# Expert weights laid out by numpy, so that each half slot is one transfer of 1 MB

## The reference

```
logits = (t @ w_router).astype(jnp.float32)
top_val, top_idx = lax.top_k(logits, TOP_K)
...
for e in range(N_EXPERTS):
    out = out + gates[:, e:e + 1] * swiglu(t, e_gate[e], e_up[e], e_down[e])
```

## Time and profile before

| What | Before |
|---|---|
| median of 3 runs | 2481.01 us (2480.24 to 2481.51) |
| profiled execution: its time, its span | 2482.85 us, 2481.6 us |
| mean granted TensorE clock | 0.994 |
| TensorE matmul busy | 2404.3 us, 97% |
| TensorE weight load busy | 1709.1 us, 69% |
| VectorE, ScalarE busy | 1046.6 us (42%), 808.7 us (33%) |
| DMA packets, bytes | 335229, 641.30 MB, mean 258 GB/s |
| expert loads, us from issue to landing | 10.9 to 13.4 (512 KB), 12.6 and 13.9 (1024 KB) |

### The profile page before, as it was taken

How to read it: one execution, slowest core, us unless ns; L and a number is a source line. 1 busy time by engine, 2 the same in 40 slices (tenths; PEclk the granted TensorE clock), 3 DMA queues, 4 the chain that set the end, 5 groups by cost and what they waited for, 6 DMA issues and landing times.

```text
span 2481.6 us, 37133 instructions
## 1 busy us (share of the span) xinstructions
PE 2404.3 (97%) x16044; PEld 1709.1 (69%) x16044; DVE 1046.6 (42%) x1477; ACT 808.7 (33%) x1107; POOL 140.4 (6%) x144
## 2 busy tenths in 40 slices
PE   9999999999999988999959999999999999999998
PEld 7899886442444433444318987898988988798897
DVE  6755563010101101010116558757547546666544
ACT  5444352010010100010114435644444444644442
POOL 2200130000000000000000001000000003400000
PEclk9999999999999999999989999999999999999999
DMA  7665468999999999999995644446556546265651
GB/s 269 207 212 181 155 216 321 377 367 394 394 394 394 394 394 393 393 392 394 392 378 165 204 137 152 168 143 232 188 171 220 187 155 252 95 228 186 205 192 46
DMA packets 335229, 641.30 MB, mean 258 GB/s; under 512 B 15701, under 2 KB 128513, under 8 KB 334673
## 3 DMA queue, kind: packets, MB, share of 16 engines
q1 hardware_dynamic: 330208, 618.64, 69.4%
q0 software_dynamic: 4848, 20.20, 2.4%
HBM read 637.73 MB, written 1.05 MB: 257 GB/s over the span
## 4 chain that ended last, share of the span: by engine, by line
PE 83%; DMA 6%; SPq 5%; DVE 4%; ACT 1%; issue 1%; POOL 0%; DVEq 0%
PE bank L640 17%; PE bank L642 17%; PE bank L641 17%; PE bank L1412 11%; PE bank L1465 6%; PE bank L1430 5%; SPq L569 5%; DMA raw_hi<-in_exp_w_down_dram 3%; PE bank L1488 2%; DVE part_lo L588 1%; PE bank L1076 1%; PE bank L1047 1%; DMA turned_raw<-in_w_in_dram 1%; PE bank L1450 1%; PE bank L652 1%
## 5 line engine op out<-in xcount | busy, mean ns | idle before, releaser
L588 DVE TENSOR_TENSOR part_lo<-raw,part_hi 128x2048 fp32r<-128x2048 f32 x149 | 339.0, 2290 | 185.6 <-ACT part_hi L580 185.6
L640 PE MATMUL bank<-x_hi,turned_part_hi 128*128 128x256 f32 x1440 | 401.7, 279 | 0.0
L641 PE MATMUL bank<-x_lo,turned_part_hi 128*128 128x256 f32 x1440 | 398.9, 277 | 0.0
L642 PE MATMUL bank<-x_hi,turned_part_lo 128*128 128x256 f32 x1440 | 398.9, 277 | 0.0
L580 ACT ACTIVATE part_hi<-raw 128x2048 fp32r<-128x2048 f32 x149 | 281.5, 1908 | 45.7 <-DMA raw<-in_ffn_w_up_dram 35.3
L640 PEld LDWEIGHTS bank<-x_hi,turned_part_hi 128*128 128x128 f32 x1440 | 270.8, 188 | 6.3 <-issue 3.0
L641 PEld LDWEIGHTS bank<-x_lo,turned_part_hi 128*128 128x128 f32 x1440 | 271.0, 188 | 3.2
L642 PEld LDWEIGHTS bank<-x_hi,turned_part_lo 128*128 128x128 f32 x1440 | 270.5, 188 | 0.0
L588 DVE TENSOR_TENSOR turned_part_lo<-turned_raw,turned_part_hi 128x2048 fp32r<-128x2048 f32 x98 | 223.5, 2311 | 89.7 <-ACT turned_part_hi L580 88.6
L2699 DVE TENSOR_TENSOR h<-silu,bank 128x256 f32<-128x256 f32 x56 | 23.6, 421 | 501.5 <-ACT silu L2011 501.5
L1412 PE MATMUL bank<-raw_hi,expert_in 128*64 128x512 f32 x896 | 212.0, 594 | 10.8 <-DMA raw_hi<-in_exp_w_up_dram 10.8
(11 more groups left out here) (292 smaller groups left out, 3268.4 us busy)
## 6 DMA issues: line engine op xcount, KB each, us to landing
raw<-in_exp_w_gate_dram SPq DMA_DIRECT2D x112, 512.0 KB, 11.9
raw<-in_exp_w_up_dram SPq DMA_DIRECT2D x112, 512.0 KB, 13.4
raw_hi<-in_exp_w_gate_dram SPq DMA_DIRECT2D x112, 512.0 KB, 10.9
raw_hi<-in_exp_w_up_dram SPq DMA_DIRECT2D x112, 512.0 KB, 12.3
raw<-in_exp_w_down_dram SPq DMA_DIRECT2D x56, 1024.0 KB, 12.6
raw_hi<-in_exp_w_down_dram SPq DMA_DIRECT2D x56, 1024.0 KB, 13.9
raw<-in_ffn_w_down_dram SPq DMA_DIRECT2D x55, 1024.0 KB, 4.9
turned_raw<-in_ffn_w_gate_dram SPq DMA_DIRECT2D x70, 512.0 KB, 4.1
```

What stands on the lines that cost most here:

```text
L588: p.nc.vector.tensor_tensor(p.part_lo[t][i][:, :], p.raw[t][i][:, :], p.part_hi[t][i][:, :].bitcast(F32), ALU.subtract).then_inc(*self.spl ...
L640: nc.tensor.matmul(out, stat_hi, move_hi, start=start, stop=False, skip_group_check=True)
L641: nc.tensor.matmul(out, stat_hi, move_lo, start=False, stop=False, skip_group_check=True)
L642: return nc.tensor.matmul(out, stat_lo, move_hi, start=False, stop=stop, skip_group_check=True)
```

## The change

numpy lays the expert weights out before the program is built. `exp_w_up` now holds gate and up together as [expert, chunk, quarter, partition, 2048], and `exp_w_down` is [expert, chunk, half, partition, 2048]. The 2048 numbers are in the order in which the half slot holds them, so a load is one transfer with 8192 contiguous bytes per partition, and the 1 MB of a load is one contiguous stretch of HBM. `exp_w_gate` is no input any more. The bytes, the order of the loads, the slots and all work of the engines are as before.

```diff
-    def expert_part(self, w, q, row, cols):
+    def expert_part(self, w, q, part):
         i, p = q // NQ, self.p
         if i % N_EXP == 0:
-            return w[0][0][row:row + 256, cols].rearrange("(k p) n -> p k n", p=P)
+            return w[0, q % NQ, part]
...
-        return w[0, bass.ds(self.expert[i], 1), row:row + 256, cols].rearrange("o (k p) n -> p (o k) n", p=P)
+        return w[bass.ds(self.expert[i], 1), q % NQ, part].rearrange("o p n -> p (o n)")
...
         def up(q):
-            cols = slice(q % NQ * FE, (q % NQ + 1) * FE)
             for kq in range(4):
-                self.add((st, "up", q, kq),
-                         [(part, lambda w=w, row=kq * 256: self.expert_part(w, q, row, cols))
-                          for part, w in (("wide_gate", a["exp_w_gate"]), ("wide_up", a["exp_w_up"]))])
+                self.add((st, "up", q, kq), [("half", lambda kq=kq: self.expert_part(a["exp_w_up"], q, kq))])
...
-                         [("rows", lambda q=q, d=d: self.expert_part(a["exp_w_down"], q, q % NQ * FE + d * 256, slice(0, D)))])
+                         [("half", lambda q=q, d=d: self.expert_part(a["exp_w_down"], q, d))])
...
+def gate_up_by_chunk(gate, up):
+    both = np.stack([gate[0], up[0]]).reshape(2, N_EXP, 4, 2, P, NQ, FE)
+    return np.ascontiguousarray(both.transpose(1, 5, 2, 4, 3, 0, 6)).reshape(N_EXP, NQ, 4, P, SLOT)
...
+def down_by_chunk(down):
+    rows = down[0].reshape(N_EXP, NQ, 2, 2, P, D)
+    return np.ascontiguousarray(rows.transpose(0, 1, 2, 4, 3, 5)).reshape(N_EXP, NQ, 2, P, SLOT)
```

More of the change, by code:

```diff
@@ L557, in fetch @@
                 p.sp.wait_ge(*p.t.at(*self.before[name]))
-            wide = raw[:, :].rearrange("p (k m n) -> p k m n", k=2, m=2)
             views = {
@@ L562, in fetch @@
                 "up": raw[:, :].rearrange("p (k m n) -> p k m n", k=4, m=2)[:, :, 1, :],
-                "wide_gate": wide[:, :, 0, :], "wide_up": wide[:, :, 1, :],
+                "half": raw[:, :],
                 "rows": raw[:, :].rearrange("p (j n) -> p j n", j=2),
@@ L617, in landed_up @@
         raw, landed = self.where(name)
-        self.p.pe.wait_ge(*landed.at(name, "wide_up"))
+        self.p.pe.wait_ge(*landed.at(name, "half"))
         return raw[:, :].rearrange("p (k m n) -> p k m n", k=2, m=2)
@@ L624, in landed_down @@
         raw, landed = self.where(name)
-        self.p.pe.wait_ge(*landed.at(name, "rows"))
+        self.p.pe.wait_ge(*landed.at(name, "half"))
         return raw[:, :].rearrange("p (j n) -> p j n", j=2)
@@ L3158 @@
 _INS = ["x", "w_in", "gm_ws", "gm_bs", "gm_ln_g", "gm_ln_b", "gla_wa2", "gla_ba", "gla_norm_g", "w_out", "ln_mix_g",
-        "ln_mix_b", "ffn_w_gate", "ffn_w_up", "ffn_w_down", "router_w", "exp_w_gate", "exp_w_up", "exp_w_down",
+        "ln_mix_b", "ffn_w_gate", "ffn_w_up", "ffn_w_down", "router_w", "exp_w_up", "exp_w_down",
         "ln_ffn_g", "ln_ffn_b", "mem_2", "ln_g_2", "ln_b_2", "ffn_w_gate_2", "ffn_w_up_2", "ffn_w_down_2",
@@ L3186 @@
             a = np.ascontiguousarray(np.asarray(inputs[name])[0].T.reshape(KT, P, T).transpose(1, 0, 2))
+        elif name == "exp_w_up":
+            a = gate_up_by_chunk(np.asarray(inputs["exp_w_gate"]), np.asarray(inputs[name]))
+        elif name == "exp_w_down":
+            a = down_by_chunk(np.asarray(inputs[name]))
         elif name == "gm_ws":
```

## The result

The changed kernel takes 2436.23 us (median of 4 runs, 2433.33 to 2438.21) against 2481.09 us before (median of 4 runs on the same chip, 2480.24 to 2481.51). The ratio is 0.9819, with a 95% interval of 0.9802 to 0.9836: faster by 44.9 us, or 1.8%. The forecast was 2434.0, range 2427 to 2452. The profiled execution took 2434.55 us (span 2433.3), which is 48.3 us less than the one of before. Executions of one kernel differ by up to 5 us, so I break down the 48.3, and take 44.9 as the gain.

The account below looks back on a forecast made before the run. Expert-load DMA was taken to bound lean experts and the stage's end, TensorE the full experts. Loads at 2.52 instead of 2.68 us save 47.1 us: 2481 - 47 = 2434 us, range 2427 to 2452 for 8 in 10.

Parts of the forecast that it names:

- What bounded the kernel: Expert stage: DMA queue bounds lean experts and the stage's end; TensorE bounds full experts at 16.24 us a chunk.
- The price: Time per 1 MB expert load: 2.68 us before, 2.52 with the change, ends 2.49 and 2.55.
- slips: Expert loads: 0.02 us added to the mean load price for instruction loads and slips between.
- the direct rows of `mem`: Two `mem` loads with 8 KB rows, at 420 and 415 GB/s: 2.50 and 2.53 us for 1 MB.
- the rule weighed: Trainium skill's fixed 3 cycles per packet: an estimated 2.44 us per MB in 8 KB rows, sum 2428; not adopted.
- The ledger: Chunk-by-chunk account of the expert stage from load price and TensorE work: stage ends at 1251.6 us, 47.1 sooner.
- The edits costed at nothing: Expert stage: 224 fewer SP issues, one landing wait per half slot and more MB queued were counted as free.
- A wait of 13 us may still do that: Stage's end: the `hT` wait may still lower TensorE's clock and slow matmuls; 2 us counted on both sides.
- Rows above 4 KB gaining nothing: Rival for expert loads: 8 KB rows go like the downs, 2.57 us a load, 33 us saved, 2448; chance 0.14.
- That row length is no limit: Rival for expert loads: some common port gives 393 GB/s whatever comes, time 2481; chance 0.05.
- Reads within one contiguous MB getting in each other's way: Slower rival for expert loads: 16 engines conflict, 377 GB/s, 2.78 us a load, 26.7 us later, 2508; chance 0.05.
- TensorE bounding it all: Rival for the expert stage: loads at 2.44 us or under, 53 us and more saved, 2428 or less; chance 0.06.

Follow-up runs that it names:

- half the bytes: Changed kernel, but behind the first 18 loads each expert load brings only half its numbers, all matmuls kept, results wrong: 2418.47 us, ratio 0.9744.
- the first experiment: Changed kernel, still one transfer of a contiguous MB per load, but 2 KB rows for ups and 4 KB for downs: 2482.61 us, ratio 0.9999 to the kernel before.
- the last two changes tried: Changed kernel with half of each later expert load: 2418.47 us; changed kernel with dense-load rounding and subtraction moved later, rounding behind the last `hT` copies: 2424.26 us.
- the new order: Changed kernel with ScalarE's rounding of dense loads behind the last `hT` copies and VectorE's subtraction behind the first rows' normalisation: 2424.26 us, ratio 0.9765.

## Why the prediction was right

**What bounded the kernel.** Right. The lean experts lost their waits, the full experts kept their 16.24 us, and with half the bytes chunk 55 starts no sooner. The leads say it most directly. By the landing times, the first load of chunk 28 was there 28.6 us ahead of its use (15.5 before, forecast 28 and 16). At the end of lean expert 4 it was 8.2 us (0 before, forecast 7), and ahead of expert 7 it was 31.1 (14.8 before, forecast 28). With 4 KB rows the lead is 0 at the end of experts 4 and 7.

**The price.** Right. 2.50 for a load in the stream, 2.52 with slips were taken; the trace has 2.49 at 421 GB/s and 2.53 from the queue's bytes, and landings 2.52 us apart. The step from the difference of 2 and 4 KB rows holds over the whole span:

| bytes in a row | packets per engine and MB | GB/s | us per MB | 2.39 + 0.010 x packets |
|---|---|---|---|---|
| 1 KB | 64 | 348 | 3.01 | 3.03 |
| 2 KB (up loads before) | 32 | 387 | 2.71 | 2.71 |
| 4 KB | 16 | 409 | 2.56 | 2.55 |
| 8 KB | 8 | 421 | 2.49 | 2.47 |

(The 2 KB row is worked out from the starts in rows 4; the others are rates of a full queue. us per MB is 1.048576 MB by GB/s.) The slope from the ends is (3.01 - 2.49) / 56 = 0.0093 us, so the line from two points was steeper by 7% than this, and the direct rows of `mem`, which I preferred to its 2.47, were nearer. Against the rule weighed: 9.3 ns a packet are 2.6 times the 3 cycles of the Trainium skill's "DMA: Bandwidth & Descriptors", Why small descriptors are slow (an estimate of 3.5 ns at the page's 850 MHz), so the trace goes against it for this queue. What a packet's fixed time is spent on, no run here shows.

**The ledger.** Right in kind, with its terms off by 1 to 4 us, which partly cancel. Its "expert 1 begins at 519.3 as now" was wrong: it begins at 515.8 (517.0 when run again). Its chunk 55, 702.0 us later, is 704.5 us later in the trace. Of these 2.5 us, 0.5 are in expert 1. From chunk 14 to 55 the ledger has 622.9; the kernel with half the bytes, which hardly waits for loads, took 624.2 (597.3 to 1221.5), so TensorE's own time was summed 1.3 us too short; and the changed kernel took 624.9 (595.4 to 1220.3), 0.7 more. The wait for `hT` came at 14.0 where 13 stood. The stage ends at 1251.4 (forecast 1251.6), because these errors cancel: that part of the closeness is luck. The parts that the forecast names, 39.5 and 5 to 6 us, leave some 2 of its 47.1 without a name. The trace has 2.9 us there, the waits between the up groups of chunk 55, which are gone. The median fell by 44.9 and not by 47.1, which is within what single executions differ.

**The edits costed at nothing.** Right: one transfer for two is worth 0, as the first experiment shows. The queue did take more at once, 8.2 MB outstanding on average from 515 to 1180 us and up to 12, instead of 4.7, and it harmed nothing.

**The end.** "A wait of 13 us may still do that", the slow matmuls behind the wait, was right: the group behind it took 3.48 us, and the clock averages 0.84 in the stretch above.

**The rivals.** Rows above 4 KB gaining nothing fell: 8 KB rows run at 421 GB/s where 4 KB rows run at 409, worth 15 to 18 us. That row length is no limit fell with four row lengths at four rates. The same page's Specifications, which put line rate at 512 B and up, are contradicted by 348, 387, 409 and 421 GB/s. Reads within one contiguous MB getting in each other's way fell with 420 to 422 in nine slices. TensorE bounding it all at 53 us and more did not come, but it is near: only the end of the stage still waits, and the last two changes tried show that it is worth 16 to 18 us with the loads cheaper still, and 10 with another order.

What stays open: why TensorE stands idle in chunk 0, and by how much. The profile names no releaser for it, so it isn't shown to be a wait for a load. Where the granted clock fell there, TensorE had just stood idle for 2.29 us (the kernel before, and the same rows in one transfer) or 2.94 (1 KB rows; a pause of 2.72 us just before it in that run brought no fall). With 4 or 8 KB rows it was 0.49 to 1.98 us, with half the bytes 2.05, and the clock didn't fall. The idle time differs between two executions of the changed kernel too (0.49 and 0.94), and no run changed it alone.

## What to carry to other kernels

Where a stage is bound by its loads, measure GB/s for each row length that the program already has, however short the stretch: two lengths gave the cost of a packet, and that carried to half and to twice as many packets. Then carry the new price through the stage chunk by chunk: here 6% cheaper loads were worth 45 us because lean experts took loads faster than they came, and half the bytes on top of it found only the end of the stage to act on. Look last at what stands in program order ahead of a small copy: moving the work that waits for loads behind it gave another 10 us without touching a transfer.

## What the runs showed beyond that

- The cost of a packet is a straight line from 8 to 64 packets per engine and MB, and neither the number of transfers (336 or 672) nor their contiguity shows beside it.
- The queue holds more MB with fewer packets, and with fewer transfers, but not in proportion (here a transfer counts from the start of its issue to its landing). Issued and not yet landed were, on average from 515 to 1180 us, 3.9 MB with 1 KB rows, 5.8 with the rows of before in one transfer (4.7 in the kernel before), 7.2 with 4 KB rows (5.7 in two transfers), and 8.2 with 8 KB rows, where slots were the limit for over 300 us. Issue to landing grew from a median of 13 us to 21, which harmed nothing here, as the loads stayed in their order.
- A wait of TensorE cost more than its length. In the `hT` wait of the changed kernel the granted clock fell to 0.5 and stayed there until 1244.5 us, so the group of eight behind it took 3.48 us instead of 1.9. In the new order it fell in the wait for `x_lo`, and the matmuls behind that lost some 2 us.
- Chunk 0 took 13.2 us in one execution of the changed kernel and 13.7 in another, and the stage began 0.8 us later in the second. So in a breakdown of one pair of profiles a part of one or two us need not be the change's.
